# Fill products on TensorE in the head of a Hymba layer step, the first weight unit ahead of a modulation group, and a root with a reciprocal in the first norm

## Chip, cores and metric

The kernel runs on one core of one Trainium2 chip. The metric is the device time of one execution in microseconds. Less is better. Everything is float32 in memory; the large products run as three single-pass products on split operands (below).

## What is computed

One step of a hybrid decoder layer for 256 prompt tokens and 8 x 8 sample tokens (320 columns in all) with 2048 channels. What the change touches is at the very start: the modulation vectors from `c`, the first RMSNorm, and the first use of the FFN weights.

```python
def _rmsnorm(x, g):
    xf = x.astype(jnp.float32)
    y = xf * lax.rsqrt(jnp.mean(xf * xf, axis=-1, keepdims=True) + EPS) * g.astype(jnp.float32)
    return y.astype(x.dtype)

def _swiglu(h, wg, wu, wd):
    return (jax.nn.silu(h @ wg) * (h @ wu)) @ wd

    # in _layer:
    mod = (jax.nn.silu(c) @ ada_w + ada_b).reshape(B, N_MOD, 1, D_MODEL)
    sh1, sc1, gt1, sh2, sc2, gt2, sh3, sc3, gt3 = [mod[:, i] for i in range(N_MOD)]
    h = _rmsnorm(x, g1) * (1 + sc1) + sh1
    x = x + 0.5 * gt1 * _swiglu(h, f1g, f1u, f1d)
    # then the mixer (RG-LRU and window attention) and a second SwiGLU, each with its norm and gate
```

## The kernel before, in words

Raw Bass: each engine has its own instruction list, written by hand, and all order between engines is by semaphores.

Weights. A weight of 1024 x 128 (or 512 x 256) values is a **unit** of 512 KB. SyncE (SP) loads unit `u` into one of four `raw` slots; ScalarE (ACT) rounds it to `hi` and VectorE (DVE) writes the rest, `lo` (both are `split(u)`); TensorE (PE) multiplies both with the split activations `h_hi`, `h_lo` (`products`, lines 564 to 566, three products of 320 columns). SP may load unit `u` once `lo_done` has reached `u - 3`.

Modulation. `ada_w` comes as 36 **groups** of eight **parts**, 512 KB each, in eight slots. `mod_unit(part, group)` (lines 568 to 576) multiplies one part with the transposed `c`: four products of 256 columns on four column strips of the array. A slot may be loaded again when `mod_used` says that its part has been multiplied. When a group is complete, ACT copies its sums out (`copy_group`, line 1040), PE transposes them (`mod_turn`), and DVE adds the bias (`add_mod`, lines 1424 and 1426).

The head, in the order of PE's list: transposes of `c`; then for `u` from 0 to 7 the transposes of two blocks of `x` (`turn_x`, line 550; DVE copies each out, line 1521; ACT squares it, line 1053; GpSimd (POOL) sums the squares, lines 1950 and 1953) and part `u` of group 0; the transposes of the small parameters and of group 0; the eight parts of group 1, with the sum over the partitions (`sum_of_squares(0)`, line 611, a product of ones with the sums) behind part 1; and the transpose of group 1. Then the FFN weights begin: four quarters of eight units (`quarter_unit`), with four parts of a modulation group ahead of every second unit.

ACT's list there: 16 squares, `copy_group(0)`, `split(0)`, the logarithm of the mean square, `copy_group(1)`, the exponential with factor -0.5 that gives `rstd`, then its share of `modulate` (lines 1069 and 1073). DVE's: 16 copies, the parameters, `add_mod(0)`, `split(0)`, `add_mod(1)`, `scale` (line 1437), `modulate` (lines 1445, 1452, 1456). In it the sample columns wait for POOL (`samples`, lines 1963 to 1976). `h_ready` counts the blocks of activations that are ready; a quarter unit needs four.

SP's list: `x`, group 0, group 1, units 0 to 3, group 2, units 4 to 7, and then half a group and two units in turn. The change leaves it as it is.

Of the kernel before, what the change touches and what calls it, by code (L numbers as in the profile page):

```python
# [31 lines left out]
ACT = mybir.ActivationFunctionType  # L32
# [4 lines left out]
P = 128  # L37
D = 2048
# [5 lines left out]
T = SEQ + SAMP  # L44
# [20 lines left out]
MODS = 8  # L65
# [31 lines left out]
Q = KB // 4  # L97
# [4 lines left out]

SUM_AT = MODS + 1


EARLY = (11, 13)
# [1 line left out]
SET_UP = 2  # L110
# [58 lines left out]
def build(nc, io):  # L169
    ctx = ExitStack()  # L170
    with ctx:
# [17 lines left out]
        ones = sb("ones", [P, P])[:, :]  # L189
# [23 lines left out]
        h_samp, at = carve(at, KB, SAMP)  # L213
        mod_row, at = carve(at, 256)
        rstd, at = carve(at, T)
        ln_ms = rms_t = rstd
        sum_sq, at = carve(at, T)
        sq, at = carve(at, 2, T)
        mod_raw_2, ffn_end = carve(at, MODS // 2, UNIT)
# [1 line left out]
        part, _ = carve(0, 2, CB, T)  # L221

        x_tok, _ = carve(0, 3, D)
        c_tok, _ = carve(3 * D, D)
# [321 lines left out]
        def _(pe):  # L546
# [21 lines left out]
            def mod_unit(part, group):  # L568
                pe.wait_ge(mod_landed[part], group * 16 + 16)
                if part == 0 and not (isinstance(group, int) and group == 0):  # L570
                    pe.wait_ge(mod_row_ready, group)
                for j in range(2):
                    for h in range(2):
                        rows = slice(32 * (2 * j + h), 32 * (2 * j + h + 1))
                        last = mm(psum[rows, B_MOD, 0:256], c_t[:, 2 * part + j, :],  # L575
                                  mod_slot(part)[:, j * 512 + h * 256:j * 512 + (h + 1) * 256], start=(part == 0), stop=(part == 7))
                last.then_inc(mod_used, 1)

            def mod_turn(group):

                pe.wait_ge(mod_row_ready, group + 1)
                if not isinstance(group, int) or group > 0:
                    pe.wait_ge(mod_done, group)
                for j in range(2):
                    last = turn(psum[:, B_MODT, j * P:(j + 1) * P], mod_row[:, j * P:(j + 1) * P], P)
                last.then_inc(mod_turned, 1)


            pe.wait_ge(ident_in, 16)
            pe.wait_ge(c_silu, 1)  # L590
            for k in range(KB):
# [30 lines left out]
            for u in range(FIRST):  # L622
                if u < MODS:
                    turn_x(2 * u)
                    turn_x(2 * u + 1)
                if u == 0:
                    pe.wait_ge(c_ready, 1)
                mod_unit(u % MODS, u // MODS)
                if u == MODS - 1:
                    turn_parameters()  # L630
                    pe.wait_ge(prm_ready, 1)
                    mod_turn(0)
                if u == SUM_AT:
                    sum_of_squares(0)
            mod_turn(1)

            def quarter_unit(q, i):
                u = 8 * q + i
                g = G_F1 + 2 * u
                arrive(u, None)  # L640
                for m in range(2):
                    free_bank(g + m, None)
                for j in range(Q):
                    k = q * Q + j
                    pe.wait_ge(h_ready, k + 1)
                    for m in range(2):
                        last = products(bank(g + m), u, j, 2 * P, m * P, h_hi[:, k, :], h_lo[:, k, :], j == 0, j == Q - 1)
                last.then_inc(unit_done, 1)

            for q in range(QUARTERS):  # L650
                first, second = 2 * q + 2, 2 * q + 3
                for i in range(8):
                    if i % 2 == 0:
                        for n in range(4):
                            mod_unit(i % 4 * 2 + n, first if i < 4 else second)
                    quarter_unit(q, i)
                    if i == 2:
                        mod_turn(first)
                    if i == 6:
                        mod_turn(second)  # L660
# [275 lines left out]
            n = 4  # L936
# [83 lines left out]
        def _(act):  # L1020
# [3 lines left out]
            def chain(instruction):  # L1024

                chained[0] += 1
                instruction.then_inc(act_chain, 1)
                act.wait_ge(act_chain, chained[0])

            def split(u, turns=None):  # L1030

                n = unit_floats(u)
                act.wait_ge(landed[u % RAW], plus(16 * (u // RAW + 1), turns, 16))
                run(hi_slot(u)[:, 0:n], raw_slot(u)[:, 0:n], ACT.Copy).then_inc(hi_done, 1)  # L1034
# [13 lines left out]
            def square(m, n, ready, count):  # L1048

                act.wait_ge(ready, count)  # L1050
                if n * KB + m >= 2:
                    act.wait_ge(summed, SUMMED[n] + m - 1)
                run(sq[:, m % 2, :], x[:, m, :], ACT.Square).then_inc(squared, 1)  # L1053
# [23 lines left out]
            def copy_group(group):  # L1077
                act.wait_ge(mod_used, group * MODS + MODS)
                copy_mod()

            for k in range(KB):
                square(k, 0, dve_freed, k + 1)
            copy_group(0)
            split(0)
            run(warm, eps, ACT.Ln)
            act.wait_ge(ms_ready, 1)
            chain(run(ln_ms, psum[:, B_NORM, 0:T], ACT.Ln, bias=eps, scale=1.0 / D))
            copy_group(1)
            run(rstd, ln_ms, ACT.Exp, scale=-0.5).then_inc(rstd_ready, 1)
            modulate(0, 0, 0, Q)  # L1090
            for u in range(1, SPLIT):
                split(u)
# [303 lines left out]
        def _(dve):  # L1396
# [9 lines left out]
            def split(u, turns=None):  # L1406

                n = unit_floats(u)
                dve.wait_ge(hi_done, plus(u + 1, turns, RAW))
                v.tensor_tensor(lo_slot(u)[:, 0:n], raw_slot(u)[:, 0:n], hi_slot(u)[:, 0:n],  # L1410
                                ALU.subtract).then_inc(lo_done, 1)
# [55 lines left out]
                                ALU.add).then_inc(samp_ready, 1)  # L1467

            def reciprocal(n):
                dve.wait_ge(rms_ready, n)  # L1470
                v.reciprocal(rstd, rms_t).then_inc(rstd_ready, 1)  # L1471

            def modulate(n, sc, sh, first, end, u=None):
                if n:
                    reciprocal(n)
                for k in range(first, end + 2):
                    if u is not None and k - 1 in EARLY:
                        finished(u + EARLY.index(k - 1))
                        split(u + EARLY.index(k - 1) + SPLIT)
                    if n and k - 2 >= first:  # L1480
                        lo_part(n, sh, k - 2)
                    if k < end:
                        normed(n, sc, k)
                        if n and k % Q == 0:
                            samples(n, sh, k // Q)
                    if n == 0 and k - 2 >= first:
                        lo_part(n, sh, k - 2)
# [33 lines left out]
                v.tensor_copy(x[:, k, :], bank(k)).then_inc(dve_freed, 1)  # L1521
            parameters()
            add_mod(0, 0)
            split(0)
            add_mod(1, Q)
            scale(0, 1, 0, Q, 2)
            modulate(0, 1, 0, 0, Q)
            for u in range(1, SPLIT):
                split(u)

# [565 lines left out]
```

## Time and profile before

| | |
|---|---|
| Time before, median of 3 runs | 2394.24 us (2391.93 to 2394.41) |
| The profiled execution | 2393.35 us, its span 2391.6 us (1.75 us lie outside the span) |
| Mean granted TensorE clock | 0.996 |
| Busy share of the span | PE 98%, DVE 50%, ACT 35%, POOL 6% |
| HBM traffic | 481 MB, 201 GB/s over the span |
| Idle time of PE in the first 60 us | 11.2 us until the identity has landed, then 3.3 us for parts of `ada_w`, 0.9 us and 0.6 us for copies |

The page cuts the span in 40 equal slices of 59.8 us, so the whole head is in the first. For it the trace has finer views: the timeline (instructions of an engine in order of time, with the idle time before them and what released it), the chain of waits (what ended last at each moment, followed back from the end), and windows (busy time, granted clock and DMA share of any stretch). A float32 product has two records for each matmul of the program. PE counts as busy from a record's start to its end, so a busy PE may be a slow one: the duration of the same instruction at two places tells more.

### The profile page before, as it was taken

To read this page: it belongs to the slowest core of one execution; us is meant where nothing else is said; L and a number is where in the kernel's file an instruction comes from. 1 tells how busy PE (TensorE), PEld (TensorE's weight loads), DVE (VectorE), ACT (ScalarE), POOL (GpSimd) and SP (SyncE) were. 2 spreads that over 40 slices of the span, in tenths; PEclk is the share of its full clock that TensorE was granted. 3 is DMA by queue.
4 is the path that set the end of the run, shared out by engine and by line. 5 is a ranking of instruction groups with operands and counts; after the bars stand their busy time and mean duration, and the time that the engine had idled before them with its cause. 6 is when DMAs were issued, how large, how long until landed. Compare 5 with 4: busy or idle time off the path is not lost.

```text
span 2391.6 us, 45647 instructions
## 1 busy us (share of the span) xinstructions
PE 2352.2 (98%) x17264; PEld 2254.7 (94%) x17264; DVE 1204.8 (50%) x2084; ACT 838.5 (35%) x1132; POOL 152.6 (6%) x176
## 2 busy tenths in 40 slices
PE   7999999999999999999999998999999999999998
PEld 3888999999999999999999998999999999999998
DVE  3665334434533545457676746454454454456344
ACT  3332222223222232235576634333232333333334
POOL 3000000000000000021031211000000000000003
PEclk9999999999999999999999999999999999999999
DMA  9999998898998857874544454555554555554553
GB/s 317 351 336 343 294 272 262 264 270 266 274 281 267 258 160 226 256 221 123 145 133 127 133 149 123 144 156 143 148 157 137 155 156 142 142 163 144 147 153 105
DMA packets 680253, 481.00 MB, mean 201 GB/s; under 512 B 15349, under 2 KB 603785, under 8 KB 679801
## 3 DMA queue, kind: packets, MB, share of 16 engines
q1 hardware_dynamic: 678080, 473.10, 66.3%
q0 software_dynamic: 1776, 6.26, 0.8%
q8 instruction: 60, 0.98, 0.2%
q10 hardware_dynamic: 306, 0.40, 0.1%
q14 instruction: 31, 0.25, 0.0%
HBM read 476.53 MB, written 5.13 MB: 201 GB/s over the span
## 4 chain that ended last, share of the span: by engine, by line
PE 93%; DVE 3%; ACT 1%; issue 1%; DMA 1%; SPq 0%; DVEq 0%; ACTq 0%
PE ps L564 29%; PE ps L566 28%; PE ps L565 28%; PE ps L575 5%; PE ps L550 1%; DMA mod_raw<-in_ada_w 1%; DVE lo L1410 1%; DVE work L1726 0%; DVE work L1772 0%; DVE work L1728 0%; ACT hi L1034 0%; DVE work L1471 0%; ACT work L1277 0%; DVE work L1892 0%; ACT work L1241 0%
## 5 line engine op out<-in xcount | busy, mean ns | idle before, releaser
L564 PE MATMUL ps<-h_hi,hi 128*128 128x320 f32 x3456 | 1077.5, 312 | 9.6 <-DVE h_lo L1456 8.6
L566 PE MATMUL ps<-h_hi,lo 128*128 128x320 f32 x3456 | 1069.3, 309 | 0.0
L565 PE MATMUL ps<-h_lo,hi 128*128 128x320 f32 x3456 | 1069.2, 309 | 0.0
L1410 DVE TENSOR_TENSOR lo<-raw,hi 128x1024 fp32r<-128x1024 f32 (+1 forms) x608 | 732.0, 1221 | 486.7 <-ACT hi L1034 485.9
L1034 ACT ACTIVATE hi<-raw 128x1024 fp32r<-128x1024 f32 (+1 forms) x608 | 625.5, 1050 | 1001.3 <-PE ps L566 874.0
L564 PEld LDWEIGHTS ps<-h_hi,hi 128*128 128x128 f32 x3456 | 650.2, 188 | 25.7 <-issue 23.7
L565 PEld LDWEIGHTS ps<-h_lo,hi 128*128 128x128 f32 x3456 | 650.2, 188 | 0.7
L566 PEld LDWEIGHTS ps<-h_hi,lo 128*128 128x128 f32 x3456 | 650.0, 188 | 0.0
L564 PE MATMUL ps<-a_hi,hi 128*128 128x320 f32 x1376 | 426.7, 310 | 1.3 <-DVE a_lo L1587 1.3
L566 PE MATMUL ps<-a_hi,lo 128*128 128x320 f32 x1376 | 425.2, 309 | 0.0
L565 PE MATMUL ps<-a_lo,hi 128*128 128x320 f32 x1376 | 425.1, 309 | 0.0
L564 PEld LDWEIGHTS ps<-a_hi,hi 128*128 128x128 f32 x1376 | 258.3, 188 | 6.8 <-issue 4.9
L565 PEld LDWEIGHTS ps<-a_lo,hi 128*128 128x128 f32 x1376 | 258.3, 188 | 0.0
L566 PEld LDWEIGHTS ps<-a_hi,lo 128*128 128x128 f32 x1376 | 258.3, 188 | 0.0
L1569 DVE SCALAR_TENSOR_TENSOR x<-ps,mod,x 128x256 f32 (+1 forms) x208 | 100.4, 483 | 227.1 <-PE ps L566 226.2
L1580 DVE SCALAR_TENSOR_TENSOR work<-work,ps 128x320 f32<-128x320 f32 x78 | 38.1, 488 | 280.3 <-ACT work L1114 272.1
L1114 ACT ACTIVATE work<-ps 128x320 f32<-128x320 f32 x78 | 34.1, 439 | 340.0 <-PE ps L566 340.0
L1950 POOL COPY work<-work 128x320 f32<-128x320 f32 x4 | 3.1, 782 | 1303.3 <-ACT work L1053 851.4
L1953 POOL TENSOR_TENSOR work<-work 128x320 f32<-128x320 f32 x57 | 71.7, 1257 | 136.2 <-ACT work L1053 68.4
L575 PE MATMUL ps<-mod_raw,c_t 128*32 128x256 f32 x1152 | 75.2, 398 | 3.3 <-DMA mod_raw<-in_ada_w 3.3
L575 PE MATMUL ps<-work,c_t 128*32 128x256 f32 x1152 | 71.4, 387 | 0.0
L575 PEld LDWEIGHTS ps<-mod_raw,c_t 128*32 128x32 f32 x1152 | 33.4, 112 | 31.3 <-issue 8.6
(221 smaller groups left out, 877.5 us busy)
## 6 DMA issues: line engine op xcount, KB each, us to landing
raw<-in_ffn_w_gate SPq DMA_DIRECT2D x172, 512.0 KB, 4.1
raw<-in_ffn_w_up SPq DMA_DIRECT2D x172, 512.0 KB, 5.0
raw<-in_ffn_w_down SPq DMA_DIRECT2D x160, 512.0 KB, 4.8
mod_raw<-in_ada_w SPq DMA_DIRECT2D x144, 512.0 KB, 8.2
work<-in_ada_w SPq DMA_DIRECT2D x144, 512.0 KB, 8.2
raw<-in_w_in SPq DMA_DIRECT2D x56, 512.0 KB, 3.8
raw<-in_w_out SPq DMA_DIRECT2D x32, 512.0 KB, 3.8
raw<-in_ffn_w_down SPq DMA_DIRECT2D x16, 384.0 KB, 2.9
```

Of the source, the lines that this page charges most:

```text
L550: return nc.tensor.transpose(out, in_, ident[0:n, 0:n])
L564: mm(out, w_hi, r_hi, start=first, stop=False)
L565: mm(out, w_hi, r_lo, start=False, stop=False)
L566: return mm(out, w_lo, r_hi, start=False, stop=last)
L575: last = mm(psum[rows, B_MOD, 0:256], c_t[:, 2 * part + j, :], mod_slot(part)[:, j * 512 + h * 256:j * 512 + (h + 1) * 256], start=(part = ...
L1034: run(hi_slot(u)[:, 0:n], raw_slot(u)[:, 0:n], ACT.Copy).then_inc(hi_done, 1)
L1114: run(silu_g[:, step % 2, :], bank(g), ACT.Silu).then_inc(silu_ready, 1)
L1410: v.tensor_tensor(lo_slot(u)[:, 0:n], raw_slot(u)[:, 0:n], hi_slot(u)[:, 0:n], ALU.subtract).then_inc(lo_done, 1)
L1569: v.scalar_tensor_tensor(out=xm[:, 0:SEQ], in0=src[:, 0:SEQ], scalar=gate[:, 0:1], in1=xm[:, 0:SEQ], op0=ALU.mult, op1=ALU.add)
L1580: v.scalar_tensor_tensor(out=prod[:, step % 2, :], in0=silu_g[:, step % 2, :], scalar=0.5, in1=bank(g + 1), op0=ALU.mult, op1=ALU.mult).th ...
L1950: g.tensor_copy(sum_sq, sq[:, 0, :]).then_inc(summed, 1)
L1953: g.tensor_tensor(sum_sq, sum_sq, sq[:, m % 2, :], ALU.add).then_inc(summed, 1)
```

## The change

Four edits.

1. PE gets `keep_busy(bank, times)`: products of the 128 x 128 tile of ones with itself, written to a PSUM bank that nothing reads then. 32 of them stand at the very start (they wait only for the two memsets of `set_up`), one ahead of each of the 16 parts of groups 0 and 1, and 8 behind `mod_turn(1)`.
2. `SUM_AT` goes from `MODS + 1` to `MODS + 4`: the sum over the partitions stands behind part 4 of group 1 and not behind part 1.
3. Unit 0 stands ahead of the first four parts of group 2 on PE and not behind them.
4. In the first norm ACT does a square root and DVE the reciprocal, in place of ACT's logarithm and exponential. The table of the root is loaded behind the squares and ahead of `copy_group(0)`. `split(0)` moves: on ACT behind `copy_group(1)`, on DVE behind the second block of `modulate`.

```diff
-SUM_AT = MODS + 1
+SUM_AT = MODS + 4
+WARM_UP = 32
...
-        ln_ms = rms_t = rstd
+        rms_1 = rms_t = rstd
...
+            def keep_busy(bank_of, times):
+
+                for _ in range(times):
+                    mm(psum[:, bank_of, 0:P], ones, ones, start=True, stop=True)
+
+            pe.wait_ge(set_up, SET_UP)
+            keep_busy(B_NORM, WARM_UP)
             pe.wait_ge(ident_in, 16)
...
                 if u == 0:
                     pe.wait_ge(c_ready, 1)
+                keep_busy(B_PT, 1)
                 mod_unit(u % MODS, u // MODS)
...
             mod_turn(1)
+            keep_busy(B_PT, 8)
...
                 for i in range(8):
-                    if i % 2 == 0:
+                    if i % 2 == 0 and (q or i):
                         for n in range(4):
                             mod_unit(i % 4 * 2 + n, first if i < 4 else second)
                     quarter_unit(q, i)
+                    if q == 0 and i == 0:
+                        for n in range(4):
+                            mod_unit(n, first)
...
                 square(k, 0, dve_freed, k + 1)
+            root_table()
             copy_group(0)
+            act.wait_ge(ms_ready, 1)
+            run(rms_1, psum[:, B_NORM, 0:T], ACT.Sqrt, bias=eps, scale=1.0 / D).then_inc(rms_ready, 1)
+            copy_group(1)
             split(0)
-            run(warm, eps, ACT.Ln)
-            act.wait_ge(ms_ready, 1)
-            chain(run(ln_ms, psum[:, B_NORM, 0:T], ACT.Ln, bias=eps, scale=1.0 / D))
-            copy_group(1)
-            run(rstd, ln_ms, ACT.Exp, scale=-0.5).then_inc(rstd_ready, 1)
             modulate(0, 0, 0, Q)
...
             def reciprocal(n):
-                dve.wait_ge(rms_ready, n)
+                dve.wait_ge(rms_ready, n + 1)
                 v.reciprocal(rstd, rms_t).then_inc(rstd_ready, 1)
...
-            def modulate(n, sc, sh, first, end, u=None):
+            def modulate(n, sc, sh, first, end, u=None, between=None):
...
+                    if between is not None and k == first + 2:
+                        split(between)
...
             add_mod(0, 0)
-            split(0)
+            dve.wait_ge(rms_ready, 1)
+            v.reciprocal(rstd, rms_1).then_inc(rstd_ready, 1)
             add_mod(1, Q)
             scale(0, 1, 0, Q, 2)
-            modulate(0, 1, 0, 0, Q)
+            modulate(0, 1, 0, 0, Q, between=0)
```

Place one is TensorE at the start of the program. Before (line 550 is a transpose, line 575 a product of a modulation part, each part four of them):

```order
L550 MATMUL ps<-ident,work 128x9 x16
L550 MATMUL ps<-ident,work 128x128 x2
L550 MATMUL ps<-ident,work 128x64
L550 MATMUL ps<-ident,work 128x128 x2
L550 MATMUL ps<-ident,work 128x64
L575 MATMUL ps<-mod_raw,c_t 32x256 x4
```

The change, same place (its line numbers are higher by one there: 551 is the transpose, 576 the part, 593 the product of ones):

```order
L593 MATMUL ps<-ones 128x128 x32
L551 MATMUL ps<-ident,work 128x9 x16
L551 MATMUL ps<-ident,work 128x128 x2
L551 MATMUL ps<-ident,work 128x64
L551 MATMUL ps<-ident,work 128x128 x2
L551 MATMUL ps<-ident,work 128x64
L593 MATMUL ps<-ones 128x128
L576 MATMUL ps<-mod_raw,c_t 32x256 x4
```

32 products of ones stand ahead of everything, and one more ahead of each part, between the transposes of `x` and the part's own products.

Place two is TensorE from the last parts of group 1 to the first unit of FFN weights. Before (line 611 is the sum over the partitions, line 564 the first product of a unit):

```order
L575 MATMUL ps<-mod_raw,c_t 32x256 x8
L611 MATMUL ps<-work,ones 128x320
L575 MATMUL ps<-mod_raw,c_t 32x256 x8
L575 MATMUL ps<-work,c_t 32x256 x16
L550 MATMUL ps<-ident,work 128x128 x2
L575 MATMUL ps<-mod_raw,c_t 32x256 x16
L564 MATMUL ps<-h_hi,hi 128x320
```

The change, from part 4 of group 1 on (line 619 is now the sum):

```order
L593 MATMUL ps<-ones 128x128
L576 MATMUL ps<-work,c_t 32x256 x4
L619 MATMUL ps<-work,ones 128x320
L593 MATMUL ps<-ones 128x128
L576 MATMUL ps<-work,c_t 32x256 x4
...
L551 MATMUL ps<-ident,work 128x128 x2
L593 MATMUL ps<-ones 128x128 x8
L565 MATMUL ps<-h_hi,hi 128x320
```

Each part has a product of ones ahead of it, the sum has moved three parts back, and the first unit follows the transposes with only eight products of ones between; the 16 products of group 2 that stood there come behind the unit.

Place three is ScalarE between its squares and its first activations. Before (lines 1085 and 1087 are the logarithm, 1089 the exponential, 1034 a split, 1040 the copy of a group):

```order
L1053 ACTIVATE work<-x 128x320 x16
L1040 ACTIVATE work<-ps 128x256
L1034 ACTIVATE hi<-raw 128x1024
L1085 ACT_TABLE_LOAD
L1085 ACTIVATE small<-small 128x1
L1087 ACTIVATE work<-ps,small 128x320
L1040 ACTIVATE work<-ps 128x256
L1089 ACT_TABLE_LOAD
L1089 ACTIVATE work<-work 128x320
L1069 ACTIVATE h_hi<-work,mod 128x256
```

The change (1069 is the root's table and first use, 1099 the root, 1053 the copy, 1047 the split, 1082 the activations):

```order
L1066 ACTIVATE work<-x 128x320 x16
L1069 ACT_TABLE_LOAD
L1069 ACTIVATE small<-small 128x1
L1053 ACTIVATE work<-ps 128x256
L1099 ACTIVATE work<-ps,small 128x320
L1053 ACTIVATE work<-ps 128x256
L1047 ACTIVATE hi<-raw 128x1024
L1082 ACTIVATE h_hi<-work,mod 128x256
```

One table load stands now ahead of the copy of group 0, the second one is gone from behind the copy of group 1 (a load ahead of a small exponential behind `split(5)` is new), and the split of unit 0 stands last.

## Rows read from the trace of the kernel before

**Rows 1.** The page: busy us, share of the span and instructions of each engine.

```profile
PE 2352.2 (98%) x17264; PEld 2254.7 (94%) x17264; DVE 1204.8 (50%) x2084; ACT 838.5 (35%) x1132; POOL 152.6 (6%) x176
```

**Rows 2.** Chain of waits in the head: start us, us, what.

```profile
2.29 13.12 DMA mod_raw<-in_ada_w
...
18.46 1.01 PE ps L575 x8
19.47 1.83 PE ps L550 x6
...
39.39 1.87 PE ps L575 x16
41.26 1.37 PE ps L611 x2
...
43.77 8.28 DMA mod_raw<-in_ada_w
```

**Rows 3.** Timeline of PE: start us, us, instruction, [idle before <-releaser].

```profile
11.19 1.87 PE L550 MATMUL ps<-ident,work 9*128 9x9 f32 x16 [11.19 <-DMA ident<-in_identity]
43.52 1.90 PE L575 MATMUL ps<-work,c_t 128*32 128x256 f32 x32
46.00 0.44 PE L550 MATMUL ps<-ident,work 128*128 128x128 f32 x2 [0.57 <-ACT work L1040]
48.02 0.64 PE L575 MATMUL ps<-mod_raw,c_t 128*32 128x256 f32 x8 [1.59 <-DMA mod_raw<-in_ada_w]
53.10 0.64 PE L564 MATMUL ps<-h_hi,hi 128*128 128x320 f32 x1
56.45 0.30 PE L564 MATMUL ps<-h_hi,hi 128*128 128x320 f32 x1
61.81 1.93 PE L575 MATMUL ps<-work,c_t 128*32 128x256 f32 x32
71.14 1.93 PE L575 MATMUL ps<-mod_raw,c_t 128*32 128x256 f32 x32
```

**Rows 4.** Windows: stretch, then busy PE, PEld, DVE, ACT, POOL; PEclk, DMA share, GB/s.

```profile
30.00:36.00 6.00, 6.00 (x36) 2.27 (x28) 2.29 (x5) 1.89 (x4) 3.75 (x5) 1.00 0.61 193
36.00:40.00 4.00, 3.07 (x23) 1.58 (x19) 1.26 (x6) 0.86 (x2) 1.42 (x2) 1.00 0.71 243
49.50:50.00 0.50, 0.50 (x8) 0.03 (x5) 0.39 (x1) 0.36 (x2) 0.11 (x1) 0.58 1.04 385
60.00:70.00 10.00, 10.00 (x88) 8.88 (x88) 8.38 (x28) 3.48 (x5) 0.00 (x0) 1.00 1.05 359
```

**Rows 5.** Timeline of PE in the mixer and at the end, at the full clock.

```profile
1188.61 0.38 PE L901 MATMUL ps<-work 128*128 128x128 f32 x2
1188.83 0.39 PE L902 MATMUL ps<-work 128*128 128x128 f32 x2
...
2379.70 4.15 PE L550 MATMUL ps<-ident,x 128*128 128x128 f32 x36
```

**Rows 6.** Windows at the end of the program, columns as in rows 4.

```profile
2386.00:2388.00 2.00, 0.00 (x0) 0.00 (x0) 0.00 (x0) 0.00 (x0) 0.00 (x0) 0.93 0.98 343
```

**Rows 7.** Timelines of POOL, ACT and DVE in the head and at the second norm.

```profile
35.70 1.87 POOL L1953 TENSOR_TENSOR work<-work 128x320 f32<-128x320 f32 x2 [0.98 <-ACT work L1053]
42.61 1.28 ACT L1085 ACT_TABLE_LOAD   x1
45.56 0.38 ACT L1040 ACTIVATE work<-ps 128x256 f32<-128x256 f32 x1 [1.03 <-PE ps L575]
50.55 0.48 DVE L1456 SCALAR_TENSOR_TENSOR h_lo<-work,mod,h_hi 128x256 fp32r<-128x256 f32 x1
51.57 1.27 DVE L1456 SCALAR_TENSOR_TENSOR h_lo<-work,mod,h_hi 128x256 fp32r<-128x256 f32 x3
59.70 1.06 ACT L1034 ACTIVATE hi<-raw 128x1024 fp32r<-128x1024 f32 x1 [4.65 <-DMA raw<-in_ffn_w_gate]
1101.06 2.15 DVE L1471 RECIPROCAL work<-work 128x320 f32<-128x320 f32 x1 [0.56 <-ACT work L1060]
```

## The prediction, on record before the changed kernel was run

> **What bounds the kernel now.** The page first: PE is busy for 98% of the span [rows 1]. From 53 us to the last products PE hardly waits, so what the change can win is an earlier arrival at the unit work, and all that is won there should last to the end. The rest of the reading is of the first 75 us.
>
> The chain of waits says what holds the head: transfers until 15.41, then PE itself with a period of 2.84 us (1.01 for a part of `ada_w`, 1.83 for six transposes), and transfers of group 2 again until 52.05 [rows 2]. The period is the point. Four parts of the same kind take 1.90 us at 43.52, 0.47 each against 1.01 [rows 2, 3], and transposes run at 0.115 us each at the end (36 in 4.15) against 1.83 / 6 = 0.305 in the head [rows 2, 5]. So PE runs the head at the lower of its two levels, 1.2 GHz, although the granted clock reads 1.00 in the windows there [rows 4]: that column shows no change of level before its first one. By the durations PE reaches 2.4 GHz behind two parts and the sum of squares, at about 42.6 [rows 2, 3], falls back at 49.58 (granted 0.58 over 49.5 to 50) [rows 4], which is 4.2 us after the last part of group 1 at 45.42, and rises again at 56.4, 3.3 us into the first unit's products [rows 3].
>
> The slow head also starves the transfers: their share is 0.61 in 30 to 36 us and 0.71 in 36 to 40, where it is 1.05 when they are pressed [rows 4], because a slot of `ada_w` is free only when its part has been multiplied.
>
> **The change, part by part.** *Products of ones.* No row has this very product, but L901 to L902 is a 128 x 128 float32 product every 0.22 us at the full clock [rows 5]. At half clock I take twice that, 0.44; the sum of squares gives the upper end, 1.37 x 128 / 320 = 0.55 [rows 2]. The 32 at the start begin at about 1.2 us. If the rise takes about 4 us (3.3 at 53.10), some 9 are slow and 23 fast: 4 + 5 = 9 us, done at 10.3. PE waits until 11.19 for the identity anyway [rows 3], so they cost nothing; with the dear price and a late rise they end near 12.5, which the wait for the first part until 15.41 still covers.
>
> *The stretch of the x transposes.* If the clock stays up, a period is 0.22 + 0.47 + 6 x 0.115 = 1.38 us instead of 2.84. A part can't land faster than 0.524 MB / 359 GB/s = 1.46 us [rows 4], so parts of group 0 end at 15.5 + 7 x 1.46 + 1 = 26.7 in place of 36.4. Then POOL is late: it adds a block of squares in 0.935 us [rows 7], 16 of them from 15.0 to 29.5. ACT's squares wait for it (two buffers), the last ends at about 28.9, and behind it now stand the root's table load, 1.28, a small activation (0.2) and the copy of group 0, 0.38 [rows 7]: 30.9. The transposes of group 0 end at 31.5; PE has idled 4 us and I assume that it has fallen back.
>
> *Group 1.* Part and fill cost 0.93 + 0.44 = 1.37 slow, 0.47 + 0.22 = 0.69 fast, the sum 1.37 or about half. With a rise after 5 us: 3.65 parts, then 4.35 x 0.69 + 0.7 = 3.7, together 8.7 us, so group 1 ends at **40.2** against 45.42, 5.2 us earlier. With an instant rise it is 37.7, where the last part has just landed; with none 43.8. The later place of the sum costs nothing as long as root (0.38 x 320 / 256, about 0.5) and reciprocal (2.15 [rows 7]) fit behind it: three parts with fills (2.1), copy and transposes (1.0, from 45.42 to 46.44 [rows 3]) make 3.1 against 2.7.
>
> *The first unit.* In the trace the first block is ready at 51.03 and the fourth at 52.84 [rows 7], 5.6 and 7.4 us behind the end of group 1 (51.57 + 1.27 is the fourth); neither POOL's sample chain nor DVE's order gets shorter, and the moved split of 1.2 us falls where DVE waits for the samples (0.2 us at most). The eight fills run in that wait. Fast and ahead of group 2, the unit goes block by block and ends 9.4 us behind group 1, four parts 1.9, the second unit 3.5: 14.8 us. Before it was 61.81 - 45.42 = 16.4 [rows 3]. Gain 1.6. The new table load ahead of the small exponential holds DVE 1.3 us longer at about 63; the banks that it frees are wanted only behind a further unit and four parts (over 5 us), so nothing.
>
> *Sum.* 5.2 + 1.6 = 6.8 us, if the transfers follow. They regain (1.05 - 0.61) / 1.05 x 6 + (1.05 - 0.71) / 1.05 x 4 = 3.8 us [rows 4]. Unit 4 landed at 59.70 [rows 7]; three units and four parts follow it in SP's list, 7 x 1.46 = 10.2, so the last of the first half of group 3 landed near 69.9 and now lands near 66.1. Its products end 0.47 later, at 66.6, and ended at 71.14 + 1.93 = 73.07 [rows 3]: **6.5 us** is what the transfers allow, and I take that. Afterwards a half quarter takes PE 9.3 us (61.81 to 71.14 [rows 3]) and six transfers 8.8, so the gain stays. Own bounds: 5.2 (late rise in group 1) to 7.6 (faster transfers).
>
> **Does the clock stay up between 10.3 and 15.5?** This decides. In that stretch PE has transposes of `c` and one pair of `x` blocks, one fill, and waits. Against: after 45.42 two transposes (0.44 us) and one part (0.64 us) did not hold the clock, it fell at 49.58 [rows 3, 4]. For: the last 36 transposes end at 2383.85, and with nothing behind them the granted clock is 0.93 over 2386 to 2388 [rows 6], a fall at 2387.7, 3.9 us later; it did not fall earlier although PE had done nothing but transposes since 2379.70 [rows 5]. So transposes hold the clock. The Trainium skill says otherwise (TensorE: Matmul & The Clock Gate, "Part 4: PE-mode transpose"): transposes do not count as PE activity in the same way, so the full clock does not engage for them. The trace disagrees for holding the clock (3.9 us behind the last transpose) and agrees for reaching it (the head never rose from 15.5 to 38). By the page the stretch would be lost and the sum would be the first rival's; by the rows the two are close, and I lean to a held clock.
>
> **The rivals.**
>
> *A: the clock falls before the first part, and the fills only add.* Then the period is 2.84 + 0.44. The old period, with PE busy all the time, never rose; 0.44 more in 3.28 need not change that. Price: seven fills (the first hides in the wait to 15.5), 3.1 us; group 1 8.7 instead of 45.42 - 39.39 = 6.0, 2.7 us; the unit's new place -1.6: **4.2 us slower**, 2398.4. With 0.55 a fill and a group 1 without a rise up to 7 slower, with an early rise 3. It decides if PE is at the lower level at 15.5. This is the case which the page's rule gives. For it: the fall at 49.58 with about as much work in between. Against: fills and a rise just ahead of the gap.
>
> *B: the transfers don't regain their 3.8 us*, for instance since issue and landing take longer when the queue is never empty. Then the first half of group 3 lands at 69.9 as before, and only the margin in front of 73.07 - 0.47 is won: 2.7 us, 2391.5. Against: they do press at 359 GB/s when they may [rows 4].
>
> *C: the head is fast, but the first unit starts slow* because PE does only eight fills in the 5.6 us ahead of it. 24 products of 0.27 (12 of them from 53.10 to 56.45) in place of 0.15 (48 between 61.81 and 71.14, less four parts) [rows 3] end at 12.2 and not 9.4 us behind group 1: 6.8 - 2.8 = 4.0 us faster, 2390.2.
>
> **How the numbers follow.** The sum is against the profiled execution's 2393.35 us (span 2391.6); the median of the three runs is 0.9 above it. 2394.24 - 6.5 = 2387.7. Chances: forecast 0.55, A 0.25, B 0.10, C 0.10. 0.2% is 4.8 us, about what a measurement of this kernel tells from no change. Faster by more: nearly all of the forecast, 0.53. Slower by more: the dear end of A, 0.09. Within: 0.38. The forecast's own range is 2386.6 to 2389; the whole range goes from 2385.5 to 2398.8, so that it takes in B, C and the nearer half of A.
>
> **What would show it.** A part of group 0 near 0.47 us and parts 1.5 us apart from 15.5 on; a wait of PE near 27 to 31 for ACT's copy of group 0; the end of group 1 at 40; transfers with no gap between 30 and 40; the first unit at 46 with products 0.15 apart; a wait for parts of group 3 near 62 to 66. Wrong if parts are 3.3 us apart (A), if the first unit's products are 0.27 apart (C), or if PE waits for group 3 until 70 (B). A slower place behind 75 us would be a mechanism I have not seen.

## The result, and the profile after

| | before | the change |
|---|---|---|
| Median | 2393.65 us (6 runs, 2391.93 to 2395.42) | 2404.76 us (6 runs, 2403.74 to 2405.78) |
| Ratio to before | 1 | 1.0044, 95% interval 1.0034 to 1.0054 |
| Span of the profiled execution | 2391.6 us | 2403.0 us |

The change is 11.1 us slower. The forecast was 6.5 us faster, and its range ended at 2398.8. The head goes the way of rival A, at more than twice its price.

Timeline of PE in the changed kernel, columns as in [rows 3]; L593 is the product of ones, L551 a transpose, L576 a part, L619 the sum:

```profile
1.03 8.90 PE L593 MATMUL ps<-ones 128*128 128x128 f32 x64 [1.03 <-POOL small L1925]
10.62 1.15 PE L551 MATMUL ps<-ident,work 9*128 9x9 f32 x16 [0.69 <-DMA ident<-in_identity]
12.91 1.21 PE L551 MATMUL ps<-ident,work 128*128 128x128 f32 x6 [1.15 <-DMA work<-in_x_sample]
14.06 0.49 PE L593 MATMUL ps<-ones 128*128 128x128 f32 x2
14.95 1.08 PE L576 MATMUL ps<-mod_raw,c_t 128*32 128x256 f32 x8 [0.40 <-DMA mod_raw<-in_ada_w]
...
17.79 0.79 PE L593 MATMUL ps<-ones 128*128 128x128 f32 x2
18.51 1.08 PE L576 MATMUL ps<-mod_raw,c_t 128*32 128x256 f32 x8
19.52 1.90 PE L551 MATMUL ps<-ident,work 128*128 128x128 f32 x6
21.35 0.79 PE L593 MATMUL ps<-ones 128*128 128x128 f32 x2
...
49.66 0.49 PE L593 MATMUL ps<-ones 128*128 128x128 f32 x2
50.07 0.64 PE L576 MATMUL ps<-work,c_t 128*32 128x256 f32 x8
50.64 0.81 PE L619 MATMUL ps<-work,ones 128*128 128x320 f32 x2
...
60.67 0.38 PE L565 MATMUL ps<-h_hi,hi 128*128 128x320 f32 x1 [3.73 <-DVE h_lo L1468]
...
80.86 1.93 PE L576 MATMUL ps<-mod_raw,c_t 128*32 128x256 f32 x32
```

The burst does what it should: it ends at 9.93, and the transposes of `c` behind it take 1.15 us, against 1.87 [rows 3]. PE waits 0.69 us ahead of them, 1.15 us behind them and 0.40 us ahead of the first part, and this part already takes 1.08 us again. From there on the period is 18.51 to 22.07, 3.56 us, against 2.84 [rows 2], and the difference is the fill: from its start to that of its part 18.51 - 17.79 = 0.72 us.

Windows of the changed kernel, columns as in [rows 4]:

```profile
12.00:14.00 2.00, 1.08 (x6) 0.67 (x6) 0.85 (x3) 0.00 (x0) 0.00 (x0) 1.00 1.05 324
14.00:16.00 2.00, 1.60 (x12) 0.54 (x11) 0.58 (x2) 0.94 (x2) 1.13 (x2) 0.60 1.05 375
30.00:36.00 6.00, 6.00 (x28) 2.95 (x24) 1.75 (x4) 1.41 (x3) 2.48 (x4) 0.50 0.43 125
36.00:40.00 4.00, 4.00 (x22) 1.84 (x25) 1.20 (x3) 1.12 (x3) 2.16 (x3) 0.50 0.52 174
48.00:50.00 2.00, 2.00 (x20) 0.75 (x12) 0.00 (x0) 0.00 (x0) 0.00 (x0) 0.86 1.10 359
```

The granted clock falls to its lower level, 1.2 GHz, at 14.4 us (0.60 over two microseconds: 0.4 us at 2.4 GHz), 4.5 us behind the last product of the burst, and comes back at 48.6, with parts and fills back to back since 43.7. Where [rows 4] had a transfer share of 0.61 and 0.71, the same windows now have 0.43 and 0.52: a slower head frees the slots of `ada_w` still later.

Where the time went, by the starts in both traces: the end of group 0's parts 36.44 to 40.92 (+4.5), from there to the end of group 1 another +4.3 (45.42 to 54.22), from there to group 3's first parts +0.9 (71.14 [rows 3] to 80.86): 9.7 us, which still stand at the reciprocal of the second norm (1101.06 [rows 7], now 1110.76). The rest of the 11.4 us between the two spans arises behind 1110 us; the last section says where.

### The profile page after: what moved, and what is told of

The parts are those of the page before. It is cut to its first block, busy times and chain, and to the rows that moved or that the text cites. A ratio compares the mean times of both kernels' runs of the same rounds, so it can differ in the third digit from the quotient of the medians.

```text
span 2403.0 us, 45869 instructions
## 1 busy us (share of the span) xinstructions
PE 2371.9 (99%) x17376; PEld 2272.9 (95%) x17376; DVE 1207.2 (50%) x2085; ACT 837.3 (35%) x1131; POOL 152.5 (6%) x176
## 4 chain that ended last, share of the span: by engine, by line
PE 93%; DVE 4%; ACT 1%; issue 1%; DMA 1%; SPq 0%; DVEq 0%; ACTq 0%
PE ps L565 29%; PE ps L567 28%; PE ps L566 28%; PE ps L576 6%; PE ps L551 1%; DVE lo L1422 1%; DMA mod_raw<-in_ada_w 1%; PE ps L593 0%; DVE work L1741 0%; DVE work L1787 0%; DVE work L1743 0%; ACT hi L1047 0%; DVE work L1483 0%; ACT work L1289 0%; DVE work L1907 0%
## 5 line engine op out<-in xcount | busy, mean ns | idle before, releaser
L1595 DVE SCALAR_TENSOR_TENSOR work<-work,ps 128x320 f32<-128x320 f32 x78 | 38.1, 488 | 280.8 <-ACT work L1126 272.7
L576 PE MATMUL ps<-mod_raw,c_t 128*32 128x256 f32 x1152 | 74.1, 394 | 0.4 <-DMA mod_raw<-in_ada_w 0.4
L576 PE MATMUL ps<-work,c_t 128*32 128x256 f32 x1152 | 72.1, 387 | 0.0
L576 PEld LDWEIGHTS ps<-work,c_t 128*32 128x32 f32 x1152 | 35.7, 111 | 25.0 <-issue 3.0
```

What stands on the lines that cost most here:

```text
L1595: v.scalar_tensor_tensor(out=prod[:, step % 2, :], in0=silu_g[:, step % 2, :], scalar=0.5, in1=bank(g + 1), op0=ALU.mult, op1=ALU.mult).th ...
```

## The experiments

Eleven kernels, each timed in five rounds beside the kernel before. The medians of before in the three sessions were 2393.86, 2394.78 and 2394.55 us. Each session had another chip, so kernels of different sessions are better compared by their ratios to before than by their medians. The first session has the runs up to the bridge, the second the four behind it, the third the last three.

**Theory:** TensorE is back at 1.2 GHz before the first part, and there and in group 1 each fill stands on the path with its own time. **Rivals:** the new order (first unit, sum, split, root) costs the time; or the burst does harm itself.

### Without the 16 fills ahead of the parts

```diff
-                keep_busy(B_PT, 1)
                 mod_unit(u % MODS, u // MODS)
```

> The change without the 16 products of ones ahead of the parts of groups 0 and 1 (the 32 at the start and the 8 behind group 1 stay). Clock theory (TensorE is back at 1.2 GHz before the first part, and each fill then costs its 0.73 us): the period of the x transposes goes from 3.57 back to 2.84 us, 7 x 0.73 = 5.1 us, and group 1, 10.5 us with fills, takes 6 to 7.5: 2395 to 2397 us. Order theory (the loss sits in the new place of the first unit and in root and reciprocal): 2403 or more, since the fills then hide in waits.

Measured: 2396.74 us, ratio 1.0009 (1.0000 to 1.0018), 8.0 us under the change. The period is 2.84 us again. The sixteen fills are eight of the eleven microseconds, and the order theory falls for these eight. The trace adds something: here the burst ends at 10.7 and the granted clock is 1.00 until 16.0 us, so the first part still ran at 2.4 GHz (0.71 us at 15.56), and the clock fell right behind it. A full clock at the first part is thus not enough.

### Without the burst

```diff
             pe.wait_ge(set_up, SET_UP)
-            keep_busy(B_NORM, WARM_UP)
```

> The change without the 32 products of ones at the start. Clock theory: their full clock is gone by 14.5 us in any case, so nothing changes in the head: 2404 to 2406 us, parts still 3.57 us apart. Burst theory (the early products themselves do harm, by using up the right to the full clock or by holding back the transposes of c): 2399 or less.

Measured: 2405.56 us (5 runs), ratio 1.0046 (1.0032 to 1.0060) beside the change's 1.0044, parts 3.56 us apart. The 32 products win nothing and cost nothing that can be measured: their full clock is lost before the first part.

### Without any fill

All three calls of `keep_busy` taken out.

> The change without any product of ones: what is left are the first unit's new place, the later sum, and root with reciprocal. Clock theory: these cost or win little by themselves (the first unit should win 1.6 us with a full clock and lose 1 to 2 at the half clock, which it has without the eight fills): 2393 to 2397 us, parts 2.84 us apart. Order theory: most of the 11 us is here, 2402 or more.

Measured: 2396.94 us, ratio 1.0012 (1.0003 to 1.0021). The other three edits alone cost 3 us against before; that is more than nothing, and two runs below take most of it apart.

### A bridge over the gap

```diff
             last.then_inc(c_turned, 1)
+            keep_busy(B_NORM, 5)
...
-                keep_busy(B_PT, 1)
+                keep_busy(B_PT, 1 if u else 4)
```

> The change with 5 more products of ones behind the transposes of c and 4 in place of 1 ahead of the first part, to bridge the 5 us in which the clock fell. Clock theory with my forecast's second half (one fill in a period holds the full clock once it is up): parts 1.4 to 1.9 us apart from 15 us on, the transfers without a gap between 26 and 42 us, 2386 to 2390 us. Rival (one fill in a period is not enough, the clock falls between the parts): parts 3.57 us apart from 18 to 22 us on, 2400 to 2404 us.

Measured: 2393.24 us, ratio 1.0002 (0.9991 to 1.0012): eight more products make the kernel 11.5 us faster than the change. Timeline of PE:

```profile
11.01 1.15 PE L551 MATMUL ps<-ident,work 9*128 9x9 f32 x16 [0.66 <-DMA ident<-in_identity]
12.09 1.38 PE L593 MATMUL ps<-ones 128*128 128x128 f32 x10
13.31 1.15 PE L551 MATMUL ps<-ident,work 128*128 128x128 f32 x6
14.40 1.16 PE L593 MATMUL ps<-ones 128*128 128x128 f32 x8
15.48 0.64 PE L576 MATMUL ps<-mod_raw,c_t 128*32 128x256 f32 x8
...
19.67 0.49 PE L593 MATMUL ps<-ones 128*128 128x128 f32 x2
20.09 0.64 PE L576 MATMUL ps<-mod_raw,c_t 128*32 128x256 f32 x8
20.66 1.21 PE L551 MATMUL ps<-ident,work 128*128 128x128 f32 x6
21.80 0.49 PE L593 MATMUL ps<-ones 128*128 128x128 f32 x2
...
48.46 0.38 PE L565 MATMUL ps<-h_hi,hi 128*128 128x320 f32 x1 [3.73 <-DVE h_lo L1469]
...
53.76 1.93 PE L576 MATMUL ps<-mod_raw,c_t 128*32 128x256 f32 x32
```

The clock holds (granted 1.00 until 49.4, within the first unit). The period is 2.13 us: fill 0.42, part 0.57, six transposes 1.14. So the mechanism of the forecast is there, but the time is only that of before, not the 2386 to 2390 expected. The trace is 2.5 us ahead at group 3's first parts (68.66 against 71.14 [rows 3]) and 2.4 at the second norm; of this 1.4 are lost between the second and the third norm, as the last section shows. One of the eleven executions took 2405.91 us at a mean clock of 0.990 (the others 0.995 or 0.996), the time and the clock of the unbridged change: there the clock seems to have fallen in the gap all the same, though that execution has no trace.

### The bridge without any other fill ahead of a part

```diff
-                keep_busy(B_PT, 1 if u else 4)
+                keep_busy(B_PT, 0 if u else 4)
```

> The bridged kernel (2393.2 us) without any fill behind the first part: 5 behind the transposes of c and 4 ahead of part 0 stay, as do the 32 and the 8. If transposes and parts alone hold the full clock, the period goes from 2.13 to about 1.7 us and group 1 from 8.3 to about 4.5: 2386 to 2388 us, perhaps with the transfers as the new limit. If one fill in a period is what holds the clock, it falls among the first parts: 2.84 us apart again, 2395 to 2398 us.

Measured: 2390.61 us, ratio 0.9986 (0.9978 to 0.9995). Between the two expectations, and the trace has both: the period is 1.71 us at the full clock, and then the clock is lost in the wait for ACT's copy of group 0 (granted 0.70 over 30 to 31 us and 0.50 behind it).

```profile
26.28 1.21 PE L551 MATMUL ps<-ident,work 128*128 128x128 f32 x6
27.42 0.64 PE L576 MATMUL ps<-work,c_t 128*32 128x256 f32 x8
27.99 0.82 PE L551 MATMUL ps<-ident,work 128*128 128x128 f32 x5
32.20 0.66 PE L551 MATMUL ps<-ident,work 128*128 128x128 f32 x2 [3.40 <-ACT work L1054]
32.79 3.64 PE L576 MATMUL ps<-mod_raw,c_t 128*32 128x256 f32 x32
```

Transposes and parts hold the clock without any fill. The Trainium skill says (TensorE: Matmul & The Clock Gate, "Part 4: PE-mode transpose") that transposes don't count as PE activity in the same way. This trace doesn't decide it, since a part stands behind every six transposes; of the traces here only the 36 transposes at the end, with nothing between them [rows 5, 6], speak against it, for holding the clock. Four parts at the half clock then take 3.64 us. (One of the eleven executions shows a mean clock of 0.944, at 2395.41 us; there is no trace of it.)

### The bridge without the fills of group 1

```diff
-                keep_busy(B_PT, 1 if u else 4)
+                keep_busy(B_PT, (4 if u == 0 else 1) if u < MODS else 0)
```

> The bridged kernel without the eight fills of group 1 alone. At the full clock a fill among the parts cost 0.42 us and made its part 0.57 in place of 0.47, with nothing to wait for: 8 x 0.5 = 4 us less, 2389 to 2390 us, group 1 in about 4.5 us. If the parts have to wait for their transfers there (a fill then hides), 1 us or less: 2392 to 2393 us.

Measured: 2389.66 us, ratio 0.9985 (0.9974 to 0.9997), 3.6 us under the bridged kernel; in the traces group 3's first parts start 3.9 us earlier (64.74 against 68.66). The price in group 1 is right: eight fills are 4 us where there is nothing to wait for. (One of twelve executions at 2404.96 us and clock 0.988, as above.)

### The same with a longer tail behind group 1

```diff
-            keep_busy(B_PT, 8)
+            keep_busy(B_PT, 22)
```

> As the kernel without group 1's fills, and 22 in place of 8 products of ones behind group 1, which end 0.5 to 1 us before the first block is ready. In the bridged kernel and in the change the clock fell within the first unit (5.3 us for a unit). If the longer tail holds it: 3.5 to 4.2 us for the unit, 1 to 2 us less than the kernel beside it. If not, or if the tail reaches past the first block, the same time or up to 1 us more.

Measured: 2388.55 us, ratio 0.9981 (0.9969 to 0.9994), 1.1 us under the kernel beside it, within the noise of both. In the trace the first unit is faster: it starts at 44.79 and the parts behind it at 48.55, 3.8 us a unit where the bridged kernel had 5.3 (48.46 to 53.76). But a new wait shows, on the first half of group 3:

```profile
64.37 1.61 PE L576 MATMUL ps<-mod_raw,c_t 128*32 128x256 f32 x24
66.66 0.64 PE L576 MATMUL ps<-mod_raw,c_t 128*32 128x256 f32 x8 [0.68 <-DMA mod_raw<-in_ada_w]
```

That is the limit which the prediction worked out: it had the landing near 66.1, and the trace has it at 66.6. The first half of group 3 is done at 67.3 here and at 66.7 in the trace of the kernel beside it, so in these two traces the faster unit wins nothing by then, and the 1.1 us between the medians are not shown to come from it. (One of twelve executions at 2405.11 us and clock 0.988, as above.)

### No fills, with the split of unit 0 in its old places

```diff
             copy_group(0)
+            split(0)
             act.wait_ge(ms_ready, 1)
...
             copy_group(1)
-            split(0)
...
             add_mod(0, 0)
+            split(0)
             dve.wait_ge(rms_ready, 1)
...
-            modulate(0, 1, 0, 0, Q, between=0)
+            modulate(0, 1, 0, 0, Q)
```

> The kernel without any fills (2396.9 us), with the split of unit 0 put back to its old places on both engines. Theory: the moved split costs about 1 us, since DVE runs it (1.65 us beside GpSimd's sample work in place of 1.23) inside the chain to the first block, which came 6.4 us behind group 1 and not 5.6: 2395.5 to 2396.2 us, first block 5.5 to 5.7 us behind group 1. Rival: the 3 us over the kernel before come from the first unit alone, which now runs wholly at 1.2 GHz and with the parts behind it: the same 2397 us.

Measured: 2396.41 us, ratio 1.0010 (1.0001 to 1.0019). In the trace the unit starts 5.7 us behind group 1 (50.65 against 44.91), where the kernel without fills had 6.6 (52.86 against 46.22): the 0.9 us are there, but of the 3 us over before they are the smaller part, and the medians (ratios 1.0010 here, 1.0012 there) don't resolve them. The two traces also differ by 1.3 us at the end of group 1, though PE does the same work in both from 15.4 us on: by the durations the clock rises near 41.7 us here and near 44.5 in the kernel without fills. Single traces of a slow head thus differ by more than a microsecond, apparently by chance.

### The kernel before with the first unit ahead, nothing else

```diff
-                    if i % 2 == 0:
+                    if i % 2 == 0 and (q or i):
...
                     quarter_unit(q, i)
+                    if q == 0 and i == 0:
+                        for n in range(4):
+                            mod_unit(n, first)
```

> The kernel before with the first unit ahead of the first four parts of group 2 and nothing else. Without fills the unit starts at the half clock and sooner by nothing (its activations come at the same moment), and the four parts, once hidden in the wait, stand behind it: 1.9 us more on the path: 1 to 2 us over the kernel before. Rival: the waits on group 2's transfers were on the path, and it wins 1 us.

Measured: 2397.38 us, ratio 1.0011 (1.0002 to 1.0020), 2.8 us over before, where 1 to 2 were expected. The rival falls. Timeline of PE:

```profile
51.12 0.61 PE L564 MATMUL ps<-h_hi,hi 128*128 128x320 f32 x1 [4.73 <-DVE h_lo L1459]
57.27 1.93 PE L575 MATMUL ps<-mod_raw,c_t 128*32 128x256 f32 x32
62.85 1.93 PE L575 MATMUL ps<-work,c_t 128*32 128x256 f32 x32
```

The unit begins 2 us sooner than at 53.10 [rows 3] but runs at 1.2 GHz until 56.4 and, though its products follow each other without a pause, takes 6.15 us; the second unit ends at 62.85, 1.0 us later than before (61.81). Without a full clock this edit loses. These 1.0 us are what the head explains; of the 2.6 us between the two spans, 1.4 more arise between the second and the third norm, where the trace of before is one of three quick ones (last section). No run has the later sum or the root with its reciprocal alone. The kernel with the split in its old places has both beside the new place of the unit, and is no slower than this one (1.6 us over its own before), so they don't seem to cost time.

### The kernel before with the bridged fills, nothing else

```diff
+            def keep_busy(bank_of, times):
...
+            pe.wait_ge(set_up, SET_UP)
+            keep_busy(B_NORM, 32)
             pe.wait_ge(ident_in, 16)
...
             last.then_inc(c_turned, 1)
+            keep_busy(B_NORM, 5)
...
+                if u == 0:
+                    keep_busy(B_PT, 4)
                 mod_unit(u % MODS, u // MODS)
```

> The kernel before with the bridged fills alone (32 at the start, 5 behind the transposes of c, 4 ahead of part 0), nothing else of the change. Theory: the held clock is the whole gain, and the order edits are not needed for it; the period is 1.71 us and group 1 ends by 39 to 41 us; but the first unit stays behind group 2's first half, whose last part then lands near 48 us: 5 to 7 us off the end of group 1 in any case, so 2388 to 2391 us. Rival (the edits to root and unit are needed before the faster head pays): 2392 to 2395.

Measured: 2390.12 us, ratio 0.9981 (0.9972 to 0.9990). The fast head pays by itself, 4.4 us. But a new wait eats part of it (PE's rows, then three of ACT):

```profile
35.53 1.91 PE L575 MATMUL ps<-work,c_t 128*32 128x256 f32 x32
41.59 0.69 PE L550 MATMUL ps<-ident,work 128*128 128x128 f32 x2 [4.15 <-ACT work L1050]
44.00 1.08 PE L575 MATMUL ps<-mod_raw,c_t 128*32 128x256 f32 x8 [1.72 <-DMA mod_raw<-in_ada_w]
...
38.14 1.06 ACT L1044 ACTIVATE hi<-raw 128x1024 fp32r<-128x1024 f32 x1 [7.16 <-DMA raw<-in_ffn_w_gate]
39.21 1.28 ACT L1095 ACT_TABLE_LOAD   x1
41.16 0.38 ACT L1050 ACTIVATE work<-ps 128x256 f32<-128x256 f32 x1
```

Group 1 is complete at 37.4, and PE waits 4.15 us for ACT's copy of it. In ACT's old list `split(0)` stands ahead of the copy, and unit 0 lands only after group 1, at 38.1, so 0.7 us of the wait are due to a transfer that the copy does not need. The other 3.0 us until the copy starts at 41.16 are the split itself (1.06), the load of the logarithm's table (1.28) and the logarithm, which waited behind the split though the sum was ready. The trace of the next kernel, with the split behind the copy and no such table load there, has 0.50 us. So the moved split, which costs 0.9 us in a slow head, helps a fast one, together with the root; no run parts the two.

### Fills only where TensorE waits, and the root's table behind the copy

```diff
-WARM_UP = 32
+WARM_UP = 34
...
             last.then_inc(c_turned, 1)
+            keep_busy(B_NORM, 5)
...
-                keep_busy(B_PT, 1)
+                keep_busy(B_PT, 0 if u else 4)
...
                     turn_parameters()
+                    keep_busy(B_PT, 8)
...
-            keep_busy(B_PT, 8)
+            keep_busy(B_PT, 22)
...
-            root_table()
             copy_group(0)
+            root_table()
```

> Fills only where TensorE waits: 34 at the start, 5 behind the transposes of c, 4 ahead of part 0, 8 behind the transposes of the parameters (in the wait for the copy of group 0), 22 behind group 1; none between the parts. The root's table load stands behind the copy of group 0. If parts and transposes alone hold the clock: period 1.71 us, the wait for the copy 1.5 us shorter, group 1 ends at 36 to 38 us instead of 38.1, where its last transfer lands: 2386 to 2389 us, no more than 2 us under the kernel with the long tail (2388.5), since the transfers of group 3 already bound that one. If the clock falls in the wait: 2389 to 2391.

Measured: 2387.44 us (6 runs, 2385.74 to 2387.89), ratio 0.9969 (0.9957 to 0.9981). It beats both kernels, by 7.1 us the one before in the same session.

```profile
28.63 0.82 PE L551 MATMUL ps<-ident,work 128*128 128x128 f32 x5
29.37 2.05 PE L593 MATMUL ps<-ones 128*128 128x128 f32 x16
31.26 0.38 PE L551 MATMUL ps<-ident,work 128*128 128x128 f32 x2
31.57 1.93 PE L576 MATMUL ps<-mod_raw,c_t 128*32 128x256 f32 x32
...
36.72 0.64 PE L576 MATMUL ps<-work,c_t 128*32 128x256 f32 x8 [0.73 <-DMA work<-in_ada_w]
37.87 0.44 PE L551 MATMUL ps<-ident,work 128*128 128x128 f32 x2 [0.50 <-ACT work L1055]
38.14 5.08 PE L593 MATMUL ps<-ones 128*128 128x128 f32 x44
43.83 0.38 PE L565 MATMUL ps<-h_hi,hi 128*128 128x320 f32 x1 [0.61 <-DVE h_lo L1470]
...
59.50 0.44 PE L551 MATMUL ps<-ident,work 128*128 128x128 f32 x2 [0.68 <-ACT work L1055]
```

```profile
24.00:28.00 4.00, 4.00 (x32) 2.00 (x31) 2.37 (x5) 1.88 (x4) 3.43 (x4) 1.00 1.05 387
28.00:32.00 4.00, 4.00 (x40) 3.03 (x43) 1.62 (x7) 2.78 (x5) 3.43 (x5) 1.00 1.06 388
30.00:36.00 6.00, 5.88 (x73) 3.21 (x72) 1.43 (x4) 2.75 (x5) 1.78 (x3) 1.00 1.06 377
```

The second fence holds windows of the same kernel, columns as in [rows 4]: the full clock, and from 30 to 36 us a transfer share of 1.06 where before it was 0.61. Group 1 now ends with a wait for its own last transfer (0.73 us): the head is bound by transfers.

## Why the prediction was wrong, point by point

*The reading of before* held. The head ran at 1.2 GHz, this starved the transfers, and an earlier arrival at the units lasts: the gains of the bridged kernels before 70 us (2.5 to 7.6 us at the end of group 3's first parts) stand unchanged at the second norm.

*"Does the clock stay up between 10.3 and 15.5?"* This step failed: I leaned to a held clock, and it fell at 14.4. PE did the parts of groups 0 and 1 at 1.2 GHz, and a fill cost its slow price without giving anything back. The rows were fairly read, the weight was not. The fall at 49.58 with two transposes and one part in between was the nearer case; the held clock behind 2379.70 was 36 transposes without a pause, and the gap had 0.69, 1.15 and 0.40 us of waiting in it. Behind the gap the forecast's picture is right: with eight more products in the gap, transposes and parts keep the full clock from 15.5 us on, with fills (period 2.13 us) and without (1.71). What in the gap makes the clock fall, the waits or the kind of work between them, no run separates.

*The price of a fill* failed. "At half clock I take twice that, 0.44", with a dear end of 0.55. It measured 0.72 to 0.73 at the half clock and 0.42 at the full one; 0.22 is what one product takes behind another of its kind, and between transposes and parts of another shape it stands alone. The row of the sum (1.37 us for 320 columns) had been scaled by columns, as if nothing in it were fixed.

*The sum of rival A*, 4.2 us. Its mechanism is what happened; its terms were 3.1 for the x transposes (measured 5.1 by 7 x 0.73, less 0.6 for a first part that landed sooner, so 4.5), 2.7 for group 1 (measured 4.3), and -1.6 for the first unit (measured +0.9).

*The first unit*, "gain 1.6", failed twice. The moved split was priced at 0.2 us at most and costs 0.9 (1.65 us on DVE beside POOL's sample work, inside the chain to the first block), and the eight fills end 3.7 us before the unit, so that the clock falls within it; with 22 it does not. This is rival C's mechanism for half of the unit. With a half clock the edit costs 1.0 us on the path.

*The forecast's own sum* would have been too high had the clock held. The bridged change, its true test, is at 2393.24, not 2387.7. Its period is 2.13 and not 1.46 us, since transposes among parts take 0.19 us each and not 0.115, and the fill 0.42 and not 0.22; group 1 took 8.3 us. The limit of the transfers was about right: it shows at 66.6 in the kernel with the long tail, and the last kernel, 7.1 us under its own before, reaches and passes the 6.5 us, but only with the fills moved out of the path. That the two sizes are so near is in part luck, since the terms behind the 6.5 are off in both directions.

*The pace of the transfers.* "A part can't land faster than ... 1.46 us" was a misreading: [rows 4] has 385 GB/s at 49.5 us beside the 359, and in [rows 3] the parts of group 2 come 1.36 us apart (48.02 to 52.09). This is a small term: the seven parts of group 0 land 0.7 us sooner at 1.36 than at 1.46. For the seven transfers from 60 us on, 359 GB/s is the right row. Rival B (the transfers don't regain their 3.8 us) did not come true once the head was fast: the last kernel has a share of 1.05 to 1.06 from 24 to 36 us.

*Later sum, and root with reciprocal.* Three parts and fills behind the sum covered them in the change, as predicted (reciprocal 52.05 to 54.20, `add_mod` at 55.19); without fills they don't quite (reciprocal until 47.53, the transposes that `add_mod` needs until 47.16). ACT's copy of group 0 behind the squares and the table was right in kind: the bridge without other fills waits 3.40 us there.

## What to carry to other kernels

A product that only keeps the clock up is free in a wait and costs its full, isolated time anywhere else (here 0.42 us, and 0.72 at the low clock, where it gave nothing back). Put such products where the engine waits, close the whole way from the burst to the first real work, and check the durations of the real instructions there, not the burst's. When a stage gets faster, look in each engine's list for an instruction that waits for something unrelated ahead of one that is now urgent.

## What the runs showed of the hardware that I had not expected

The granted-clock column reads 1.00 for a head that runs at 1.2 GHz if the clock was never up before: the kernel without the burst has a mean of 0.997 and the change 0.989 with the same parts 3.56 us apart. Durations of one instruction in two places settle it.

The clock's fate in a short wait differs between traces although the work around it is the same. At the wait for the second norm it stayed up in the trace of before and fell in that of the change:

```profile
1100.00:1110.00 10.00, 7.09 (x77) 5.38 (x76) 9.18 (x19) 4.72 (x10) 0.99 (x1) 1.00 0.18 55
```

```profile
1110.00:1120.00 10.00, 7.08 (x68) 5.68 (x68) 9.18 (x19) 4.78 (x10) 0.70 (x1) 0.85 0.17 54
```

The first is a window of before, the second the same place in the change. From the second norm's reciprocal to the third's it is 359.2 us in the one and 360.65 in the other. This is 1.45 of the 1.7 us that the change's trace loses behind the head. Of the thirteen traces three have 359.1 or 359.2 us (before, the long tail, and the last kernel) and ten have 360.6. I count it to the execution and not to the change, which is not shown, since each kernel has only one trace. The executions of before itself do differ by as much and with the clock, though nothing says at which place: in the second session the nine with a mean clock of 0.998 have spans of 2388.7 to 2389.7 us, the fifteen with 0.996 spans of 2391.0 to 2393.5. Whether the same chance explains the single executions near 2405 us of three bridged kernels was not tried, for want of a trace of one.
